# Loading expert weights and the second projection's weights in pieces of 1024 columns instead of 2048

## What is computed

```python
def hier_moe(h, w_group, b_group, w_exp, b_exp, w_gate, w_up, w_down):
    """Top-1 expert group, then top-2 experts inside it; gated-MLP experts."""
    ...
    combine = jnp.sum(jax.nn.one_hot(expert_id, N_EXPERTS, dtype=jnp.float32) * e_w[..., None], axis=1)
    hid = jax.nn.silu(jnp.einsum('nd,edf->nef', xt, w_gate)) * jnp.einsum('nd,edf->nef', xt, w_up)
    hid = hid * combine[:, :, None].astype(hid.dtype)
    out = jnp.einsum('nef,efd->nd', hid, w_down)

def gqa_project(h, w_qkv, g_q, g_k):
    ...
    qkv = h @ w_qkv
```

## Time and profile before

| | |
|---|---|
| Median of 3 runs (lowest to highest) | 1355.89 us (1354.52 to 1357.55) |
| The profiled execution, own time | 1360.44 us |
| Its span in the trace | 1358.6 us |
| TensorE busy (matmul) | 1251.4 us, 92% |
| Queue q1 (SP) | 180.76 MB, 34.8% of 16 engines |
| Queue q10 (ACT) | 43.78 MB, 10.2% |
| Queue q0 (POOL) | 64.59 MB, 12.1% |

### The profile page before, as it was taken

The page is one execution under the profiler, slowest core; times in us unless marked ns, Lnnn a source line. Parts: engine busy times, 40 slices in busy tenths (PEclk is TensorE's granted clock), DMA queues, the critical chain, the costliest instruction groups (busy, mean ns, idle before and its releaser), DMA issues.

```text
span 1358.6 us, 16949 instructions
## 1 busy us (share of the span) xinstructions
PE 1251.4 (92%) x5449; PEld 672.4 (49%) x5450; DVE 588.3 (43%) x1350; ACT 418.8 (31%) x845; POOL 56.1 (4%) x64
## 2 busy tenths in 40 slices
PE   5999899999989999899958998899999999899995
PEld 2554566666654474344424443455544574344441
DVE  1322355545533664222217445677734652223215
ACT  2322344444441121011123225666731111011123
POOL 0102000000000110000020000000000110000003
PEclk9999899999989999899989998899999999899998
DMA  9969999422262166999954003100040259878956
GB/s 375 401 273 412 408 409 414 160 94 95 98 215 113 42 265 212 369 361 366 374 193 176 8 1 155 38 1 1 1 158 1 91 235 332 291 273 307 378 203 241
DMA packets 77539, 290.05 MB, mean 213 GB/s; under 512 B 11705, under 2 KB 29820, under 8 KB 63004
## 3 DMA queue, kind: packets, MB, share of 16 engines
q1 hardware_dynamic: 28944, 180.76, 34.8%
q0 software_dynamic: 16640, 64.59, 12.1%
q10 hardware_dynamic: 31884, 43.78, 10.2%
HBM read 214.38 MB, written 74.73 MB: 213 GB/s over the span
## 4 chain that ended last, share of the span: by engine, by line
PE 78%; DMA 7%; DVE 4%; SPq 3%; ACTq 3%; ACT 3%; issue 2%; POOL 1%; DVEq 1%; POOLq 0%
PE ps L1959 15%; PE ps L1627 10%; PE ps L1610 10%; PE ps L1563 8%; PE ps L1988 7%; PE ps L1840 6%; DMA arena<-slot_rows 4%; PE ps L1803 4%; PE ps L2040 3%; PE ps L1905 3%; PE ps L1658 3%; PE ps L1683 3%; PE ps L1578 2%; PE ps L1796 2%; DMA arena<-in_ada_w 2%
## 5 line engine op out<-in xcount | busy, mean ns | idle before, releaser
L1959 PE MATMUL ps<-arena 128*128 (+1 forms) x560 | 251.8, 603 | 0.0
L1563 PE MATMUL ps<-const,arena 128*128 128x128 f32 (+2 forms) x1000 | 158.6, 287 | 55.2 <-DVE arena L1482 17.1
L1563 PEld LDWEIGHTS ps<-const,arena 128*128 128x128 f32 (+2 forms) x1000 | 119.6, 145 | 133.2 <-issue 44.5
L1098 DVE TENSOR_REDUCE hst<-ps 128x1 f32<-128x640 f32 (+1 forms) x160 | 114.8, 717 | 120.0 <-PE ps L1840 84.7
L1959 PEld LDWEIGHTS ps<-arena 128*128 128x128 f32 x560 | 106.2, 195 | 120.8 <-issue 120.7
L1610 PE MATMUL ps<-arena 128*128 128x512 f32 (+2 forms) x400 | 154.6, 543 | 8.1 <-DVE arena L1057 4.8
L688 ACT ACTIVATE arena<-ps 128x640 f32<-128x640 f32 (+1 forms) x160 | 99.1, 620 | 180.1 <-PE ps L1563 158.7
L1627 PE MATMUL ps<-arena 128*128 128x512 f32 x320 | 142.0, 596 | 1.4 <-issue 1.4
L1988 PE MATMUL ps<-arena 128*128 (+1 forms) x280 | 126.1, 593 | 2.2 <-ACT arena L792 2.2
L693 ACT ACTIVATE arena<-ps,hst 128x640 f32<-128x640 f32 (+1 forms) x160 | 112.8, 705 | 20.6 <-DVE hst L1098 20.5
L1610 PEld LDWEIGHTS ps<-arena 128*128 128x128 f32 x400 | 75.7, 193 | 80.1 <-issue 62.4
(11 more groups left out here) (211 smaller groups left out, 1112.5 us busy)
## 6 DMA issues: line engine op xcount, KB each, us to landing
arena<-in_moe_gu SPq DMA_DIRECT2D x64, 1024.0 KB, 9.2
arena<-in_ada_w SPq DMA_DIRECT2D x62, 768.0 KB, 11.3
slot_rows<-arena POOLq DMA_DIRECT2D x10, 4096.0 KB, 66.7
arena<-in_moe_w_down SPq DMA_DIRECT2D x32, 1024.0 KB, 12.4
slot_rows<-arena ACTq DMA_DIRECT2D x33, 512.0 KB, 9.4
arena<-slot_rows ACTq DMA_DIRECT2D x124, 128.0 KB, 9.3
arena<-mod_rows ACTq DMA_DIRECT2D x12, 512.0 KB, 7.1
arena<-in_gqa_w_qkv SPq DMA_DIRECT2D x6, 1024.0 KB, 13.4
```

What stands on the lines that cost most here:

```text
L1098: nc.vector.tensor_reduce(hst[:, b:b + 1], scores(s, step(s)[3]), AX.XY, ALU.max, negate=True)\
L1563: return nc.tensor.transpose(out, in_, ident[0:rows, 0:rows])
L1959: last = mm(bank(gu_bank(u)), e_xsT[:, nth(u, D)][:, k * P:(k + 1) * P], w(k * BANK, BANK), start=k == 0, stop=k == KD - 1)
```

## The change

The weights of experts, down matrices and `qkv` are loaded by a new helper, `in_pieces`, in DMAs of 1024 columns: 4 KB for each partition and 512 KB in all. `gu` takes four DMAs instead of two, `dn` two instead of one, each part of `qkv` four instead of two. The counts that readers wait for double (`LANDS`). Bytes, places, order and waits stay.

```diff
+PIECE = 1024
...
-    LANDS = {"gu": 32, "dn": 16}
+    LANDS = {"gu": 64, "dn": 32}
...
+        def in_pieces(sem, dst, src):
+            for a in range(0, dst.shape[1], PIECE):
+                sp.dma_start(dst[:, a:a + PIECE], src[:, a:a + PIECE]).then_inc(sem, 16)
+
         def load_gu(l, e):
-
-            half = SLOT // 2
-            for h in range(2):
-                sp.dma_start(slot_of(("gu", l, e))[:, h * half:(h + 1) * half], A["moe_gu"][l, e, :, h * half:(h + 1) * half])\
-                    .then_inc(landed(("gu", l, e)), 16)
+            in_pieces(landed(("gu", l, e)), slot_of(("gu", l, e)), A["moe_gu"][l, e])
 
         def load_dn(l, e):
-            sp.dma_start(slot_of(("dn", l, e)), A["moe_w_down"][l, e]).then_inc(landed(("dn", l, e)), 16)
+            in_pieces(landed(("dn", l, e)), slot_of(("dn", l, e)), A["moe_w_down"][l, e])
...
-            load(landed(name), slot_of(name), A["gqa_w_qkv"][b], KD)
+            in_pieces(landed(name), slot_of(name), A["gqa_w_qkv"][b])
```

## The result

The changed kernel takes 1342.46 us as the median of 7 runs (1340.28 to 1348.40); the kernel before, run beside it, 1355.79 (1352.51 to 1358.53). The two medians differ by 13.3 us. The ratio of the times, estimated from all these runs and not from the two medians, is 0.992, 95% interval 0.9898 to 0.9943: faster by 0.8%, 8 to 14 us. Forecast was 1339.5.

A forecast was written before the change was run, and what follows sets the result against it. TensorE waits for row loads in both layers' tile loops, 22.2 us in all. Gains of 8.5 (layer 0) and 7.9 (layer 1) sum to 16.4 us, taken from the 1355.89 median: 1339.5 us, range 1333 to 1352.

The forecast's parts named there:

- the turn: Both loops: queues alternate by packet; with 4 KB weight packets q10 needs 10.9 us a tile instead of 16.9.
- the signs named: Loops: even packet counts, bytes about 4 : 1, row loads under 22 us, shorter ACT issues, weights landing in 15 to 24.
- Layer 1: Its loop over tiles: the deficit stays inside weights' 11 us of slack, so the whole 7.9 us goes.
- Layer 0: Its loop over tiles: 8.5 us gained at tile 15, while 5.8 us remain as waits for weights near the end.
- a sign of being wrong: Loops: rows still taking 25 us and more, or `gate_up` waiting for weights from the loop's middle on.
- the total: Layer 0's loop: 53.4 MB at 362 GB/s take 147.6 us, plus 2.1 us for 4 KB packets.
- More DMAs at no cost: SP's queue: 96 more DMAs for experts and 6 for `qkv`, some 0.4 us each, costed at nothing.
- The estimate of 6 us more for each expert: Expert weight loads: the skill's fit, taken as if transfers ran one by one; the prediction set it against the trace.
- Full recovery: Rival, chance 0.17: both loops lose nearly all 22.2 us of waits, giving 1334 to 1336 us.
- weights take over early: Rival, chance 0.13: waits for weights eat layer 0's gain, the clock dropping after each; only layer 1's 7.9 remain: 1348.
- The price that would have made it slower: Slower rival, chance 0.10, layer 0: from 0.210 us per 4 KB packet the kernel is slower by over 2.7 us.
- No effect: Rival, chance 0.05: the DMA engines serve two adjacent 4 KB packets in one turn, giving 1356 us.

The follow-up runs named there:

- e9: Kernel before, weights still in 8 KB packets but in 512 KB DMAs that each take every second partition: 1357.5 us, ratio 1.003.
- e2: Changed kernel with gate, up and `qkv` still in 4 KB packets but in 1 MB DMAs: 1346.12 us, ratio 0.9953 to the kernel before.
- e7: Changed kernel with stores of the experts' results cut to 128 of 1024 columns: 1334.03 us, ratio 0.9838 to the kernel before.
- e8: Kernel before with stores of the experts' results cut to 128 of 1024 columns: 1352.33 us, ratio 0.9958 to the kernel before.
- e4: Kernel before with only down in 4 KB pieces, gate, up and `qkv` in 8 KB: 1349.98 us, ratio 0.9969.
- e1: Kernel before, weights still in 8 KB packets but in 512 KB DMAs of 64 adjacent partitions each: 1499.04 us, ratio 1.105.

## Why the prediction was right, and where it was off

**What bounded the kernel.** Right. The kernel before waited for rows while weights were 11 to 13 us early, and the cause was the turn, packet for packet. Shown by e9 in loops and time, by e2 in the loops and in its packet counts (the packet, not the DMA), and by e7 beside e8 (the turn, even with a total that 4 KB handles without a wait). Of the signs named, the counts, the bytes (4 : 1), the slowest row load (20.0 us, under 22) and ACT's issues came as forecast: four DMAs took ACT up to 13.00 us before and 2.52 at most in the changed kernel, but for the eight at the loop's start (5.72 us).

**Layer 1.** Forecast 7.9 us, measured 7.9. Its sum has a slip: 12.2 - 10.52 is 1.7 us a tile and not 1.3, so the deficit by tile 6 is 10 us and not 8. That is still inside the 11 us of slack, and nothing came late.

**Layer 0.** Forecast 8.5 us, measured 6.2: 8.1 us stay late instead of 5.8. Weights are waited for from 600 to 650 us, that is from tile 9 of 15, and not from 640 to 675. Waits for weights from the loop's middle on had been named as a sign of being wrong; as to when weights become late, the prediction was wrong. The term that was mis-sized is the total: 53.4 MB at 362 GB/s and 2.1 us for the packets, 149.7 us. Counted like that, 3.3 us from tile 1 to 524.0 in the kernel before and so from 518.6 in this one, they took 670.6 - 518.6 = 152.0 us: 351 GB/s. (The trace counts 54.0 MB in that stretch, 355 GB/s.) A mean over the loop also hides when the bytes are needed. Windows up to the last wait and behind it, where the row loads soon end:

```profile
518.60:649.30 130.70, 123.76 (x303) 54.63 (x301) 34.22 (x36) 16.88 (x24) 0.00 (x0) 1.00 1.03 348
649.30:670.60 21.30, 21.29 (x54) 9.71 (x55) 5.58 (x6) 1.79 (x3) 0.00 (x0) 1.00 1.03 401
```

The waits ended with tile 13, at 348 GB/s; the fast rest came too late for them. Why the total costs 2.3 us more than forecast has two explanations, and no run separates them. One is the rows: the forecast raised the price of the weight packets (0.312 for 0.305) and left that of the rows. In the old loop not every row packet stood beside a weight packet; from 590 to 592 us they ran nearly alone, at 0.060 us each. Now each costs 0.250 - 0.156 = 0.094. The other is the weights: the 0.156 us came from POOL's queue, and q1 alone in the changed kernel, from 656 to 664 us, shows

```profile
DMA packets 898, 3.28 MB, mean 410 GB/s; under 512 B 97, under 2 KB 97, under 8 KB 898
```

which is 8 x 16 / 801 = 0.160 us for a packet of 4 KB. Two of them cost 0.015 us more than one of 8 KB and not 0.007, for 304 of them 4.6 us instead of 2.1, and this alone would be the miss. A row packet in the pair of 0.250 is then left with 0.090.

**The size in time.** Forecast 16.4 us. The loops of the two profiles differ by 14.1, the medians of all runs by 13.3, and the ratio says 10.8 (8 to 14). So 2.3 us of the miss are in the loops, all in layer 0, and the rest lies between one profile and many runs. The forecast took the lateness of one profiled execution for that of all; that execution was 4.6 us above the median. Of the twelve comparisons with the kernel before, nine gain 3 to 6 us less by the ratio than in the loops of the profiles (e9 loses that much more); e4, e7 and e8 agree within 2 us. Every one of them uses the same profile of the kernel before, so the gap would fit a profile whose loops waited some us longer than they do on average. Whether they did is open, since no second profile of that kernel was taken.

**More DMAs at no cost.** Right in effect. SP's issues did become long, up to 5.64 us, since its queue now fills. But e2 with half as many DMAs for gate and up was no less late in layer 0 (10.0), and e7 with all of them was not late at all. The estimate of 6 us more for each expert, worked out from the fit in the Trainium skill, "DMA: Bandwidth & Descriptors", section "Anatomy of one DMA — SWDGE (gpsimd) path", which the page gives for GpSimd's path, did not come: from 656 to 664 us, q1 alone with pieces of 512 KB ran at 410 GB/s.

**The rivals.** Full recovery did not happen, and e7 shows a way to it: 0.46 MB less for each tile. The "weights take over early" case has a part of the truth, in tiles 9 to 13, but the clock did not drop: with waits of 2.21 us at most, the granted clock stood at 1.00 in the loop's window. The price that would have made it slower, 0.21 us for a 4 KB packet, was not reached: if rows are put at 0.060, a 4 KB packet costs 0.190 at most in the pairs of 0.250, and only beside rows; alone it costs 0.160. "No effect" was refuted by the even packet counts.

## What to carry to other kernels

Where two queues share the DMA engines, compare their packet counts and their bytes in a stretch in which both wait: if counts are even, the size of a run sets who gets the bandwidth, and smaller runs on the queue that is early speed up the one that is late, as they did here. It moves lateness and does not remove it, so look first how much slack the early one has, and stop at the size at which both are just in time. Judge the mechanism by the loop it acts on, tile by tile, and its worth by the time of many runs: here the loops of one profile promised 14 us, and the ratio of the runs gave 11.

## What the runs showed of the hardware that was not expected

- 64 adjacent partitions in a DMA: 240 GB/s in the loop with the engines busy throughout; every second partition, with the same bytes, packets and count of DMAs, 367 GB/s (e1 and e9).
- ACT's and SP's issues of a DMA become long when much is outstanding on their queue (5.23 us for one DMA of ACT before, up to 5.64 us on SP after), and hold up everything behind them on that engine, arithmetic too. Counted from the DMAs issued and the data packets begun, every issue longer than 1 us in layer 0's loop came with more than 60 packets outstanding for each DMA engine, on ACT in the kernel before and on SP in the changed one; with fewer, none took over 0.7 us.
- Two queues that both wait take turns by packets of data, also where one's DMA brings an engine 16 of them and the other's 8 (284 to 283 packets in e2).
- A 1 KB packet costs 0.060 us nearly alone and some 0.09 to 0.108 beside weights, while 4 KB stores beside 8 KB weights cost nothing extra.
